# Two retention products moved between the norms of the shared key and value

## The reference, cut to what matters

```python
z = h @ w_in[l]
qa, c_kv, iq, ik, iw, qb, kb, vb, gb = jnp.split(z, IN_OFFSETS, axis=-1)
qa = rmsnorm_2(qa.reshape(b, s, A_HEADS, HEAD_DIM_2), q_norm_w[l])
c = rmsnorm_2(c_kv, kv_norm_w[l])
ka = rmsnorm_2(c @ w_uk[l], k_norm_w[l])
va = c @ w_uv[l]
out_a = indexed_sparse_attention(qa, ka, va, iq..., ik, iw, rel_bias)
qr = rotary(qb...); kr = rotary(kb...) * HEAD_DIM_2 ** -0.5
y = chunkwise_retention(qr, kr, vr)
```

## Time and profile before

| | us |
|---|---|
| median of 3 runs | 2679.21 |
| lowest, highest | 2674.0, 2684.59 |
| the profiled execution | 2679.19 |
| its span, first to last instruction | 2677.9 |
| mean granted TensorE clock | 0.984 |

### The profile page before, as it was taken

The page is one execution under the profiler, slowest core; times in us unless marked ns, Lnnn a source line. Parts: engine busy times, 40 slices in busy tenths (PEclk is TensorE's granted clock), DMA queues, the critical chain, the costliest instruction groups (busy, mean ns, idle before and its releaser), DMA issues.

```text
span 2677.9 us, 35255 instructions
## 1 busy us (share of the span) xinstructions
PE 2586.3 (97%) x12632; PEld 2155.1 (80%) x12632; DVE 1285.1 (48%) x2488; ACT 1043.7 (39%) x1938; POOL 1265.4 (47%) x887
## 2 busy tenths in 40 slices
PE   7999999999999999999988999779999999999999
PEld 6888887887888888887866777679888888888887
DVE  4115445277666762225356777756427333333222
ACT  5335553243333332224345666466324333332120
POOL 2132223456666665444424444277246666666441
PEclk9999999999999999999998999979999999999999
DMA  3233312312222244211221122221222222216311
GB/s 131 91 95 91 95 63 103 126 56 95 79 87 79 87 158 172 79 58 49 86 79 60 56 72 74 84 68 45 112 81 75 79 87 79 87 66 249 110 47 71
DMA packets 89261, 238.47 MB, mean 89 GB/s; under 512 B 10208, under 2 KB 22784, under 8 KB 88704
## 3 DMA queue, kind: packets, MB, share of 16 engines
q1 hardware_dynamic: 89088, 236.21, 25.4%
HBM read 180.60 MB, written 51.38 MB: 87 GB/s over the span
## 4 chain that ended last, share of the span: by engine, by line
PE 79%; DVE 5%; POOL 2%; issue 2%; ACT 2%; DMA 1%; SPq 0%; ACTq 0%; DVEq 0%; POOLq 0%
PE PS L913 9%; PE PS L911 9%; PE PS L912 9%; PE PS L667 7%; PE PS L669 7%; PE PS L668 7%; PE PS L929 6%; PE PS L931 6%; PE PS L930 6%; PE PS L1181 2%; PE PS L793 2%; PE PS L1161 1%; PE PS L881 1%; PE PS L882 1%; PE PS L883 1%
## 5 line engine op out<-in xcount | busy, mean ns | idle before, releaser
L667 PE MATMUL PS<-Hh,Wl 128*128 128x512 f32 x1072 | 442.3, 413 | 17.3 <-DVE Hl L1292 11.3
L669 PE MATMUL PS<-Hh,Wh 128*128 128x512 f32 x1072 | 424.8, 396 | 0.0
L668 PE MATMUL PS<-Hl,Wh 128*128 128x512 f32 x1072 | 424.2, 396 | 0.0
L2936 POOL TENSOR_TENSOR Wl<-Wr,Wh 128x1024 fp32r<-128x1024 f32 (+1 forms) x83 | 188.6, 2274 | 413.6 <-ACT Wh L2153 413.6
L3033 POOL TENSOR_TENSOR RG<-RW,RG 128x512 fp32r<-128x512 f32 x176 | 244.6, 1393 | 142.8 <-ACT RG L2414 142.8
L1660 DVE TENSOR_TENSOR XA<-PS,XA 128x512 f32<-128x512 f32 x192 | 132.5, 691 | 329.1 <-PE PS L931 329.1
L929 PE MATMUL PS<-Hh,RG 128*128 128x512 f32 x704 | 274.4, 390 | 0.4 <-issue 0.4
L930 PE MATMUL PS<-Hl,RG 128*128 128x512 f32 x704 | 274.1, 389 | 0.0
L931 PE MATMUL PS<-Hh,RG 128*128 128x512 f32 x704 | 274.1, 389 | 0.0
L667 PEld LDWEIGHTS PS<-Hh,Wl 128*128 128x128 f32 x1072 | 207.3, 193 | 61.0 <-issue 15.1
L912 PE MATMUL PS<-Hl,RG 128*128 128x512 f32 x640 | 249.1, 389 | 0.0
(11 more groups left out here) (355 smaller groups left out, 5204.4 us busy)
## 6 DMA issues: line engine op xcount, KB each, us to landing
RW<-in_wg SPq DMA_DIRECT2D x44, 512.0 KB, 3.5
RW<-in_wu SPq DMA_DIRECT2D x44, 512.0 KB, 4.5
R<-in_wd SPq DMA_DIRECT2D x88, 256.0 KB, 3.0
hgscr<-GB SPq DMA_DIRECT2D x44, 512.0 KB, 2.6
G<-hgscr SPq DMA_DIRECT2D x40, 512.0 KB, 6.8
Wr<-in_wi SPq DMA_DIRECT2D x27, 512.0 KB, 3.3
Wr<-in_wo SPq DMA_DIRECT2D x16, 512.0 KB, 3.3
spill<-X SPq DMA_DIRECT2D x16, 512.0 KB, 2.6
```

The costliest lines, as they stand in the source:

```text
L667: pe.matmul(ps(b), k.Wl[:, s, wc], xh[:, kx, sl], start=kk == 0, stop=False)
L668: pe.matmul(ps(b), k.Wh[:, s, wc], xl[:, kx, sl], start=False, stop=False)
L669: i = pe.matmul(ps(b), k.Wh[:, s, wc], xh[:, kx, sl], start=False, stop=kk == nk - 1)
L2936: pool.tensor_tensor(k.Wl[:, s, 0:w], k.Wr[:, s, 0:w], k.Wh[:, s, 0:w].bitcast(F32), ALU.subtract).then_inc(*up("w_lo", "w_lo", u))
```

## The change

The two products of retention's first query block, (`q`, 0) half 0 and 1, are taken out of the retention loop and stand inside the norm chain, with the chain's links as slots at their k-steps. The index scores tick at pace 2 in them. The shared key's two halves get banks 2 and 7, and the values bank 2. The last links are in another order: the statistics of key half 1 stand inside the second product, those of half 0 behind it; the turns and outputs take half 1 first. VectorE and ScalarE get the same order; ScalarE copies the two results into `rr` right behind each product and readies the weight piece ahead of them. In the loops of the three engines (`q`, 0) is skipped, and with it the six ticks that its two products had on VectorE and ScalarE.

```diff
-    hn_stat("c", 1, 7, True)
+    def keys():
+        pe.wait_ge(*at("d_kv_in"))
+        for half in range(2):
+            b = (2, 7)[half]
+            take(b)
+            if half == 0:
+                pe.wait_ge(*at("hn", "c", 1))
+            pe.matmul(ps(b), k.wkv[:, 0:128], k.CT[:, half_of(half)], start=True, stop=True).then_inc(
+                *up(("full", b), "kk", half))
+
+    def values():
+        take(2)
...
+    u = next(unit)
+    product([(u, H, ("rt", "q", 0, 0), False)], 8, 0, {1: lambda: hn_stat("c", 1, 7, True), 3: lambda: hn_turn("c", 0, 2),
+                                                       6: lambda: hn_turn("c", 1, 7)}, pace=2)
     bg.tick()
...
+    product([(u, H, ("rt", "q", 0, 1), True)], 8, 1, {1: keys, 4: lambda: hn_stat("kk", 1, 7), 6: values}, pace=2)
     bg.tick()
-    for t in range(2):
-        hn_stat("kk", t, (2, 7)[t])
-        bg.tick()
-    for t in range(2):
-        hn_turn("kk", t, (2, 7)[t])
+    hn_stat("kk", 0, 2)
+    hn_turn("kk", 1, 7)
+    hn_turn("kk", 0, 2)
     bg.drain()
...
     for j in range(4):
         for c in "qkvg":
-            u = next(unit)
-            for half in range(2):
-                product([(u, H, ("rt", c, j, half), half == 1)], 8, half)
-                bg.tick()
+            if (c, j) != ("q", 0):
+                u = next(unit)
+                for half in range(2):
+                    product([(u, H, ("rt", c, j, half), half == 1)], 8, half)
+                    bg.tick()
```

VectorE and ScalarE:

```diff
+    walk(8, 2, {1: c_ms, 3: lambda: c_out(0), 6: lambda: c_out(1)}, tick)
     bank.next()
     tick()
...
+    walk(8, 2, {6: lambda: hn_root("kk", 1)}, tick)
+    bank.next()
+    tick()
+    hn_root("kk", 0)
+    for t in (1, 0):
         hn_out("kk", t, k.KA[:, half_of(t)], col("k_norm_w_2"), (2, 7)[t])
...
+    use()
+    walk(8, 2, {1: c_cast}, tick)
+    copied(k.rr, 0, ("rt", "q", 0, 0), ("rw", "q", 0, 0))
     tick()
...
+    walk(8, 2, {1: kk_in, 4: lambda: hn_root("kk", 1, 7), 6: values}, tick)
+    copied(k.rr, 1, ("rt", "q", 0, 1), ("rw", "q", 0, 1))
     tick()
...
+    hn_cast("kk", 1)
+    hn_root("kk", 0, 2)
+    hn_cast("kk", 0)
+    act.wait_ge(*at("hn", "kk", 0))
     act.wait_ge(*at("hn", "kk", 1))
     act.activation(k.KS[:, :], k.KA[:, :], ACT.Copy).then_inc(*up("prep_a", "ks_hi"))
     bg.drain()
```

More of the change, by code:

```diff
@@ L1028, in tensor @@
     bg.tick()
-    hn_stat("c", 1, 7, True)
-    bg.tick()
-    for t in range(2):
-        hn_turn("c", t, (2, 7)[t])
-        bg.tick()
-    pe.wait_ge(*at("d_kv_in"))
-    for half in range(2):
[L1037 to L1041, removed]
-        bg.tick()
[L1043 to L1047, removed]
-    bg.tick()
-    for t in range(2):
-        hn_stat("kk", t, (2, 7)[t])
-        bg.tick()
-    for t in range(2):
-        hn_turn("kk", t, (2, 7)[t])
+    def keys():
[9 more added lines that the diff above has]
+        take(2)
+        for i in range(8):
+            m = pe.matmul(ps(2)[:, 64 * i:64 * i + 64], k.CT[:, 128 * i:128 * i + 128], k.wkv[:, 128:192], start=True,
+                          stop=True)
+        m.then_inc(*up(("full", 2), "va"))
+    u = next(unit)
+    product([(u, H, ("rt", "q", 0, 0), False)], 8, 0, {1: lambda: hn_stat("c", 1, 7, True), 3: lambda: hn_turn("c", 0, 2),
+                                                       6: lambda: hn_turn("c", 1, 7)}, pace=2)
+    bg.tick()
+    product([(u, H, ("rt", "q", 0, 1), True)], 8, 1, {1: keys, 4: lambda: hn_stat("kk", 1, 7), 6: values}, pace=2)
+    bg.tick()
+    hn_stat("kk", 0, 2)
+    hn_turn("kk", 1, 7)
+    hn_turn("kk", 0, 2)
     bg.drain()
@@ L1814, in vector, with c_ms, c_out @@
     tick()
[L1815 to L1818, removed]
+    def c_ms():
+        hn_ms("c", 1, 1)
+        hn_root("c", 1, True)
+    def c_out(t):
         hn_out("c", t, k.CT[:, half_of(t)], col("kv_norm_w_2"), (2, 7)[t])
[L1820 to L1823, removed]
+    walk(8, 2, {1: c_ms, 3: lambda: c_out(0), 6: lambda: c_out(1)}, tick)
     bank.next()
     tick()
[L1826 to L1829, removed]
+    walk(8, 2, {6: lambda: hn_root("kk", 1)}, tick)
[3 more added lines that the diff above has]
+    for t in (1, 0):
         hn_out("kk", t, k.KA[:, half_of(t)], col("k_norm_w_2"), (2, 7)[t])
     dve.wait_ge(*at("ks_hi"))
-    dve.wait_ge(*at("hn", "kk", 1))
+    dve.wait_ge(*at("hn", "kk", 0))
     dve.tensor_tensor(k.KS[64:128, :], k.KA[64:128, :], k.KS[64:128, :].bitcast(F32), ALU.subtract).then_inc(*up("prep_v", "ks"))
@@ L1991, in vector @@
         for c in "qkvg":
-            for half in range(2):
-                walk(8, 3, {}, tick)
-                tick()
+            if (c, j) != ("q", 0):
+                for half in range(2):
+                    walk(8, 3, {}, tick)
+                    tick()
         bg.drain()
@@ L2725, in scalar, with c_cast, kk_in, values @@
     tick()
-    hn_root("c", 1, 7, True)
-    hn_cast("c", 1, True)
-    tick()
[L2729 to L2737, removed]
-    tick()
[L2739 to L2743, removed]
+    def c_cast():
+        hn_root("c", 1, 7, True)
+        hn_cast("c", 1, True)
+    def kk_in():
+        for half in range(2):
+            b = (2, 7)[half]
+            hn_in("kk", half, k.KA[:, half_of(half)], ps(b), b, ("kk", half))
+    def values():
+        act.wait_ge(*at("va"))
+        act.activation(k.VA[:, :, :], ps(2).rearrange("p (i n) -> p i n", i=8), ACT.Copy).then_inc(*up(("free", 2), "va_out"))
+    use()
+    walk(8, 2, {1: c_cast}, tick)
+    copied(k.rr, 0, ("rt", "q", 0, 0), ("rw", "q", 0, 0))
+    tick()
+    walk(8, 2, {1: kk_in, 4: lambda: hn_root("kk", 1, 7), 6: values}, tick)
+    copied(k.rr, 1, ("rt", "q", 0, 1), ("rw", "q", 0, 1))
+    tick()
+    hn_cast("kk", 1)
+    hn_root("kk", 0, 2)
+    hn_cast("kk", 0)
+    act.wait_ge(*at("hn", "kk", 0))
     act.wait_ge(*at("hn", "kk", 1))
@@ L2809, in scalar @@
         for c in "qkvg":
+            if (c, j) == ("q", 0):
+                continue
             use()
```

## The result

The changed kernel takes 2685.98 us (median of 20 runs, 2681.18 to 2692.11) against 2678.42 us before (20 runs beside them). The ratio is 1.003, 95% interval 1.0024 to 1.0037: slower by 7.6 us on the medians. The forecast was 2685.0 us, in a range of 2675 to 2691, with the note that no difference under 0.5% could be told from none. The interval is narrower than that: it tells this difference of 0.3% from none. The profiled execution took 2687.74 us, with a span of 2686.4.

What follows compares the result with a forecast made beforehand. TensorE, busy 97% of the span, was taken as the bound, but another queue as setting the turn of the values. 2679.2 + 0 (turn) + 4.8 (drain) + 1.0 (last stage) = 2685.0 us, range 2675 to 2691.

Steps and rivals of the forecast that it cites:

- The hole is filled: In the norm chain, the moved query products fill TensorE's waits at full clock; first key product near 1437.5, against 1446.2 before.
- rival 2: In the norm chain, the clock stays at 0.73, everything behind `KS` is 8.5 us late, total 2693.5 us; chance 0.13.
- The norm chain ends later and the table with it: At the chain's end, `KS` is ready at 1440.3 and the cosine table is issued 5.3 us later than before.
- Term one: At TensorE's turn of the values: 0 us change, since another queue sets that point.
- the 8.7 us: How much earlier the first key product starts; forecast to become a longer wait at the turn of the values, about 13.3 us.
- The table ends last: Ahead of GpSimd's first sine product, the cosine table's path ends at 1449.2, after the exchanged rows land near 1447.7.
- Interleaving regimes: The skill's advice that interleaving a kernel's regimes may gain; by that alone, minus 8.7 us at the turn of the values.
- Term two: In the search's drain before attention, six lost ticks move selection steps behind the last query turn: +4.8 us.
- Two bits in the last stage: In the first last-stage product, two search bits now add ScalarE counts: +1.0 us, between 0 and 4.9.
- terms two and three: The lost ticks' costs together: +4.8 us in the drain and +1.0 us in the last stage, 5.8 us.
- 1 (the gain comes through): At the turn of the values, it comes 4.7 or the whole 8.7 us earlier; chance 0.17.
- 3 (the drain hides): At the drain, VectorE enters earlier, with the front at 0, so the total is 2679 to 2681 us; chance 0.20.

Runs made afterwards that it cites:

- kernel 3: The changed kernel with SyncE sending query 0's eight exchanges before it waits for the shared key, ahead of the tables and the weight fetch: 2688.14 us, ratio 1.0032.
- kernel 1: The kernel before with only the six search ticks of query 0's two products taken out on VectorE and ScalarE: 2683.8 us, ratio 1.002.
- kernel 4: kernel 3 with the cosine table in two loads, the sines' half loaded and scaled early: 2683.06 us, ratio 1.002.
- kernel 2: The changed kernel with the six ticks given back by pace 2 in three products of retention group 0: 2682.68 us, ratio 1.0017.
- kernel 5: kernel 4 with the six ticks given back as in kernel 2: 2678.75 us, ratio 0.9998.
- kernel 8: kernel 4 with query 0's exchanges in the other order, half 1 first: 2680.01 us, ratio 1.0009.

## Why the prediction was right, point by point

**The hole is filled.** Right. The first key product starts 27.2 us behind the anchor; forecast 1437.5 in the time of the trace before, which is 27.0. The granted clock was 1.00 and rival 2 (0.73) did not happen. Between 1411.7 and 1439.7 TensorE was busy 24.5 us and idle 3.5; the forecast had 23.1 and 4.7, so two small errors cancel. Two things were not forecast. VectorE's multiply-add at 1415.95 took 2.55 us beside GpSimd's weight piece, the next one of that size 1.02, and c's last cast came 1.2 us later than walked. And behind the waits at the end, of 1.87 and 0.95 us, the first key product began at a granted clock of 0.53 (1439.7 to 1443.0), which only takes from the wait that follows.

**The norm chain ends later and the table with it.** Right: `KS` at 29.9 behind the anchor, forecast 29.8 (1440.3). The table landed 4.7 us behind its issue.

**Term one, 0 us at the turn.** Right in that the 8.7 us became a wait, wrong in the input that came last: the term measured +2.0 us. The step that failed is "The table ends last", with the exchanged rows that "land near 1447.7". The table came as forecast: the sine product could have started behind the cosine product at 1449.3 in the time of the trace before, forecast 1449.2. SyncE began to issue the exchanges as forecast too (1445.0 less the 2.0 us of offset, against 1442.8), but their rows released GpSimd only at 1451.4. The turn came at 1474.7, just outside the 1472 to 1474 of the forecast. From the page's part on DMAs, 1436 to 1458 after:

```profile
CS<-in_cs SPq DMA_DIRECT2D x1, 1024.0 KB, 4.7
DQ<-in_dq SPq DMA_DIRECT2D x1, 768.0 KB, 6.1
Wr<-in_wi SPq DMA_DIRECT2D x1, 512.0 KB, 7.8
K<-rr SPq DMA_DIRECT2D x8, 64.0 KB, 5.8
```

The change brought table, decay table, weight piece and exchanges within 2.5 us of each other, and the small exchanges took 5.8 us at the median, where the kernel before has 2.2. That the loads beside them are the cause is supported by two other kernels. In kernel 3 the same exchanges go out ahead of all loads:

```profile
K<-rr SPq DMA_DIRECT2D x8, 64.0 KB, 2.0
```

In kernel 1 they go out 2.0 us sooner behind the anchor than in the kernel before, right behind the weight fetch; they took 3.6 us, and the first sine product stayed at 38.7. So the rows bound, 2.07 us behind the cosine product, and not the table. Kernel 3 and kernel 4 show that both inputs had to come sooner for a gain. Of the 2.0 us, 0.6 had gone again by the last gate product of retention (258.4 behind the anchor, against 257.0); the half-clock stretch behind the wait was shorter in this execution, which need not come from the change, as the last section shows. By the run times kernel 2 puts the front at 4.6 us (2.1 to 6.7): not 0.

**Interleaving regimes.** The Trainium skill (Perfetto Trace Analysis, Optimization Strategy) says that interleaving regimes may help; counted by that alone the term was minus 8.7 us. The hole did take the products, and none of it reached the end. The measurement decides.

**Term two, +4.8 us in the drain.** Right in its mechanism: the wait before attention grew by 3.5 us. The step list is the one that was forecast, and the moved steps took 4.6 us. The steps behind them took 1.1 less than before: the scan over 768 columns 2.0 less (1.76 us here, 3.78 before), one multiply 0.9 more. In the kernel before GpSimd subtracts a weight piece beside it; after, that piece (3.57 us from 1737.24) lies beside that multiply, of `chosen(4)`, which took 1.82 in place of 0.88 us. That the overlap is the cause is read from the timelines and was not tried by itself.

**Two bits in the last stage, +1.0 us.** From the last gate copy to the last query output the trace after needs 0.9 us more (63.5 against 62.7). Consistent, from one execution each. Kernel 1 shows terms two and three together at 5.4 us (2.9 to 8.0), forecast 5.8.

**The sum.** 1.4 us up to the last gate product, 0.9 in the last stage, 3.5 in the drain and 0.8 behind it are about 6.5 us from the anchor to the end, between the profiled executions; the medians differ by 7.6. The forecast had 5.8. The rest of 1 us is inside the scatter of the runs. That the total came so near is in part luck: the front was taken too low by 1.4 us up to the last gate product, and the drain too high by 1.3.

**Rivals.** 1 (the gain comes through) did not happen; kernels 4, 5 and 8 show what it would have needed. 3 (the drain hides) fell with kernels 1 and 2.

## What to carry to other kernels

Filling a hole on the busiest engine pays only if that engine sets the next meeting point. Follow the other queues to it first: here a table load was queued behind the norm chain's last result, so the work that filled the hole made the meeting point later. When work is spread by ticks of a loop, moving an iteration out of the loop also moves as many steps of it to wherever the list is drained; six ticks were worth 3.5 to 5.9 us in four comparisons, in either direction. And a small DMA that is moved ahead of another costs its issue time in the queue, 0.6 to 0.7 us each here.

## What the runs showed of the hardware, unexpected

TensorE's stretch at the lower of its two clock levels, behind the turn of the values, did not follow the length of the wait before it. Over 5.9 us from the turn the granted clock was 0.51 behind a wait of 4.58 us and 0.69 behind 12.81 us in the changed kernel, but 0.50 behind 12.77 us in kernel 2; behind 11 us it was 0.50 in kernel 4 and 0.77 in kernel 5. So single executions differ by over 1 us at this place, and a shorter stretch in one of them is no effect of a change. Exchanges of 64 KB landed in 2.0, 2.2, 3.6 or 5.8 us at the median, by what was in flight beside them.
